# Seven-product FFN slabs with weight sums kept in device memory

## What is computed

```python
def swiglu_2(h, w_in, w_out):
    gate, up = jnp.split(h @ w_in, 2, axis=-1)
    return (jax.nn.silu(gate) * up) @ w_out

# block 1 of the first model (its FFN result is gated by the modulation, then the final norm follows)
x = x + mod_l[5] * swiglu(modulate(rmsnorm(x, ffn_norm_g[i]), mod_l[3], mod_l[4]), ffn_w1[i], ffn_w3[i], ffn_w2[i])
# a layer of the second model
x = x + 0.5 * swiglu_2(rms_norm(x, ffn1_norm[l]), ffn1_w_in[l], ffn1_w_out[l])
```

## Time and profile before

| | |
|---|---|
| Runs of before | 1642.88 us (1642.75 to 1643.07) |
| Profiled execution | 1642.93 us, span 1641.6 us |
| TensorE busy in the span | 1619.2 us (99%) |
| VectorE, ScalarE, GpSimd busy | 75%, 52%, 18% |
| DMA | 346 MB, 211 GB/s in the mean |
| TensorE clock granted | full |

### The profile page before, as it was taken

One profiled execution on the slowest core, in us unless ns is written; L12 is line 12 of the kernel. 1 busy time (PEld: TensorE's weight loads), 2 busy tenths in 40 slices (PEclk: granted clock), 3 DMA queues, 4 the chain that ended last, 5 costly groups with the idle time before them and its releaser, 6 DMA issues.

```text
span 1641.6 us, 21147 instructions
## 1 busy us (share of the span) xinstructions
PE 1619.2 (99%) x7872; PEld 1309.4 (80%) x7872; DVE 1226.6 (75%) x1476; ACT 850.7 (52%) x1062; POOL 292.8 (18%) x429
## 2 busy tenths in 40 slices
PE   6999999999999999999999999999999999999999
PEld 3776788888778888788888878888888888888887
DVE  3898778897787674766978776688667978866686
ACT  3436654435475443645656554454545647564453
POOL 0001000000002240134403002450044204003350
PEclk9999999999999999999999999999999999999999
DMA  9784398898638876577665428766676664347661
GB/s 350 242 289 169 106 318 278 309 353 264 205 123 268 272 251 196 175 232 225 200 189 180 129 80 248 224 198 220 200 215 211 216 199 158 103 129 233 215 212 52
DMA packets 250295, 346.22 MB, mean 211 GB/s; under 512 B 16160, under 2 KB 197124, under 8 KB 250192
## 3 DMA queue, kind: packets, MB, share of 16 engines
q1 hardware_dynamic: 236288, 323.00, 59.8%
q0 software_dynamic: 11472, 17.34, 4.5%
q10 hardware_dynamic: 2432, 4.51, 0.8%
HBM read 329.32 MB, written 1.05 MB: 201 GB/s over the span
## 4 chain that ended last, share of the span: by engine, by line
PE 89%; DVE 5%; ACT 3%; issue 1%; DMA 1%; SPq 0%; DVEq 0%; ACTq 0%
PE bank L491 21%; PE bank L493 21%; PE bank L492 21%; PE bank L898 5%; PE bank L903 5%; PE bank L899 5%; DMA raw<-in_ada_w 1%; DVE lo L2059 1%; PE bank L1411 1%; PE bank L1412 1%; PE bank L1414 1%; PE bank L846 1%; PE bank L1219 1%; ACT hi L1467 1%; DVE XN L2545 1%
## 5 line engine op out<-in xcount | busy, mean ns | idle before, releaser
L2059 DVE TENSOR_TENSOR lo<-raw,hi 128x2048 fp32r<-128x2048 f32 x230 | 528.2, 2300 | 194.2 <-ACT hi L1467 193.9
L1467 ACT ACTIVATE hi<-raw 128x2048 fp32r<-128x2048 f32 x242 | 462.0, 1914 | 248.0 <-PE bank L493 173.0
L491 PE MATMUL bank<-hi,XTh 128*128 128x512 f32 (+1 forms) x1424 | 558.8, 392 | 1.7 <-DVE XTl L2216 1.3
L493 PE MATMUL bank<-hi,XTl 128*128 128x512 f32 (+1 forms) x1424 | 551.4, 387 | 0.0
L492 PE MATMUL bank<-lo,XTh 128*128 128x512 f32 (+1 forms) x1424 | 550.9, 387 | 0.0
L491 PEld LDWEIGHTS bank<-hi,XTh 128*128 128x128 f32 x1424 | 267.4, 188 | 65.9 <-issue 12.5
L493 PEld LDWEIGHTS bank<-hi,XTl 128*128 128x128 f32 x1424 | 267.4, 188 | 55.2
L492 PEld LDWEIGHTS bank<-lo,XTh 128*128 128x128 f32 x1424 | 267.6, 188 | 53.8 <-issue 1.0
L3153 POOL DMA_DIRECT2D HTR<-BLK x320 | 192.4, 609 | 624.7 <-DVE BLK L2647 585.2
L898 PE MATMUL bank<-hi,HTh 128*128 128x512 f32 x400 | 156.6, 391 | 0.0
L899 PE MATMUL bank<-lo,HTh 128*128 128x512 f32 x400 | 155.7, 389 | 0.0
(11 more groups left out here) (420 smaller groups left out, 1862.8 us busy)
## 6 DMA issues: line engine op xcount, KB each, us to landing
raw<-in_ffn_w_in SPq DMA_DIRECT2D x176, 512.0 KB, 4.9
raw<-in_ffn_w SPq DMA_DIRECT2D x132, 512.0 KB, 5.0
raw<-in_ada_w SPq DMA_DIRECT2D x96, 512.0 KB, 5.5
raw<-in_ffn_w_out SPq DMA_DIRECT2D x88, 512.0 KB, 4.1
raw<-in_w_mix_in SPq DMA_DIRECT2D x52, 512.0 KB, 4.7
raw<-in_od_pw_w SPq DMA_DIRECT2D x24, 512.0 KB, 6.2
HTR<-BLK POOLq DMA_DIRECT2D x240, 48.0 KB, 3.9
raw<-in_ev_w_in SPq DMA_DIRECT2D x20, 512.0 KB, 9.8
```

The costliest lines, as they stand in the source:

```text
L491: pe.matmul(dst, xh, wh, start=start, stop=False)
L493: return pe.matmul(dst, xl, wh, start=False, stop=stop)
L1467: act.activation(hi[r][:, :], raw[g % RAW][:, :], ACT.Copy).then_inc(*up("hi", d))
L2059: dve.tensor_tensor(lo[r][:, :], raw[g % RAW][:, :], hi[r][:, :].bitcast(F32), ALU.subtract).then_inc(*up("lo", d))
```

## The change

- `FAST` takes in p = 2, the gated FFN ahead of the final norm, and `FASTS` becomes (0, 1, 3, 4, 6, 7): six of eleven down slabs in five FFNs, 30 slabs in place of 16.
- The weight sums no longer come from VectorE. GpSimd's queue makes them in a new buffer in device memory, `A["sums"][p]`, for each slab by six DMAs: two copies of 512 KB from the weight, then two accumulating DMAs of 256 KB from the weight, then one of 256 KB from the buffer to itself, then another one. Two slabs form a batch, and GpSimd waits for each of the four steps of each batch. The new function `weights_sums(p)` on GpSimd is called for p = 2 after the Fourier weights' DMAs, for p = 3 and 5 after the convolution's constants and ahead of `move_blocks(2)`, and for p = 6 and 8 after GpSimd's part of the mixers, ahead of `move_blocks(3l+5)`.
- The sums become slabs of their own in the weight stream (`sums_slab`), split like others, each behind its weight slab, which now leaves one quarter out (`fast_slab`). A down stage has 17 slabs in the stream in place of 11. SyncE waits for `sums_made` ahead of such a slab.
- `seven` uses two ring slots, with `used` raised after 9 and after 12 matmuls. The signs of the scheme change. `shared_sums` moves behind the splits of the last fast slab, and for p = 2 multiplies by the gate (`shared_added`).
- The places of the splits of `HTR` change (`FAST_SPLIT_UP`, `FAST_SPLIT_DOWN`); `SR`, `SL`, `SH` get new places in SBUF.

The diff, cut to its core:

```diff
     "hg_logs": "hg_e hg_ln hg_sig hg_z",
     "hg_squares": "hg_rows hg_sq hg_std hg_silu",
...
@@ -154,10 +155,27 @@
             return [(d[:, k, :], w[(2 * s + k) * P:(2 * s + k + 1) * P, :]) for k in range(2)]
         add(parts)
 
-    def down(name, w):
+    def fast_slab(w, s):
+        def parts(slot):
+            d = slot[:, :].rearrange("p (k n) -> p k n", k=2)
+            return [(d[:, 0, 0:512], w[2 * s * P:(2 * s + 1) * P, 0:512]), (d[:, 1, :], w[(2 * s + 1) * P:(2 * s + 2) * P, :])]
+        add(parts)
+
+    def sums_slab(p, i):
+        def parts(slot):
+            return [(slot[:, n * D:(n + 1) * D], A["sums"][p][i, :, n * D:(n + 1) * D]) for n in range(2)]
+        add(parts)
+
+    def down(name, w, p=None):
         first[name] = len(dense)
         for s in range(w.shape[0] // (2 * P)):
-            down_slab(w, s)
+            if p in FAST and s in FASTS:
+                fast_at[len(dense)] = FFNS[p], FASTS.index(s)
+                fast_slab(w, s)
+                sums_at[len(dense)] = p
+                sums_slab(p, FASTS.index(s))
+            else:
+                down_slab(w, s)
 
     def wide_slab(w, c0):
         v = row_tiles(w)
...
@@ -281,10 +299,11 @@
 SPLIT_UP = {5: (0, 1), 6: (2,), 8: (3, 4), 9: (5,), 10: (6,)}
 SPLIT_DOWN = {0: (7,), 1: (8,), 4: (9, 10)}
 
-FAST = (3, 5, 6, 8)
-FASTS = (1, 3, 5, 7)
-FAST_SPLIT_UP = {5: (0,), 6: (1, 2), 8: (4,), 9: (3, 5), 10: (6,)}
-FAST_BATCH = {n: [i for i, s in enumerate(FASTS) if s in batch] for n, batch in enumerate(BATCHES)}
+FAST = (2, 3, 5, 6, 8)
+FASTS = (0, 1, 3, 4, 6, 7)
+FAST_SPLIT_UP = {5: (2,), 6: (0, 1), 8: (5,), 9: (3, 4)}
+FAST_SPLIT_DOWN = {1: (8,), 2: (6, 7), 4: (9, 10)}
+FAST_BATCH = {n: [i for i, s in enumerate(FASTS) if s in batch] for n, batch in enumerate(BATCHES[:3])}
 FAST_COLUMNS = {6: 0, 9: 1}
 GAINS = {3: "ffn1_0", 4: "mix2_0", 5: "ffn2_0", 6: "ffn1_1", 7: "mix2_1", 8: "ffn2_1"}
 
...
@@ -440,11 +459,10 @@
         CAUSAL = tile_at("CAUSAL", [P, P + FOX_H], tmp_at + 4096)
 
         TR = tile_at("TR", [P, SLAB], tmp_at)
-        SR = tile_at("SR", [P, len(FASTS), 4, P], tmp_at + 8192)
-        SL = tile_at("SL", [P, len(FASTS), 4, P], tmp_at + 8192, F32R)
-        SH = tile_at("SH", [P, len(FASTS), 4, P], gate_at, F32R)
-        TH = XTh[:, :, :].rearrange("p k s -> p (k s)")
-        TL = XTl[:, :, :].rearrange("p k s -> p (k s)")
+        SR = tile_at("SR", [P, 8, 4, P], tmp_at)
+        SL = tile_at("SL", [P, 8, 4, P], tmp_at, F32R)
+        SH = [tile_at(f"SH{n}", [P, 2, 4, P], (gate_at, gate_at + 4096, scr_at)[n], F32R) for n in range(3)]
+        SHG = [tile_at(f"SHG{n}", [P, 2, 4, P], (tmp_at + 4096, cst_at, scr_at)[n], F32R) for n in range(3)]
         SUMS2 = SG[:, :, :].rearrange("p t n -> p (t n)")
 
         vec = A["vec"]
...
@@ -860,31 +904,32 @@
-                    return SH[:, i, n, :], SL[:, i, n, :]
+                    return sums_high_at(f, batch)[:, i - FAST_BATCH[batch][0], n, :], SL[:, sums_slot(i), n, :]
...
+                    pe.wait_ge(*at("hidden", (f, NC - 2, 1)))
+                three(bank[2][:, :], *x(0, 0), *w(0, 0), begin, end)
+                pe.wait_ge(*at("s_hi", (f, batch)))
+                pe.wait_ge(*at("s_lo", (f, batch)))
+                three(acc[0][1][:, :], *x_sum(3), *w(1, 1), begin, False).then_inc(*up("used", d))
+                ready(d + 1)
+                three(bank[3][:, :], *x_sum(0), *w_sum(0), begin, end)
+                three(acc[1][0][:, :], *x(1, 1), *w_sum(2), begin, False)
                 if begin:
                     pe.wait_ge(*at("hidden", (f, NC - 1, 1)))
-                three(bank[2][:, :], *x(0, 0), *w(0, 0), begin, end)
-                pe.wait_ge(*at("s_hi", (f, next(n for n in FAST_BATCH if i in FAST_BATCH[n]))))
-                pe.wait_ge(*at("s_lo", (f, next(n for n in FAST_BATCH if i in FAST_BATCH[n]))))
-                three(acc[0][1][:, :], *x_sum(3), *w(1, 1), False, False)
-                pe.wait_ge(*at("t_hi", (f, i)))
-                pe.wait_ge(*at("t_lo", (f, i)))
-                three(bank[3][:, :], *x_sum(0), *w_sum(0), begin, end)
                 three(bank[1][:, :], *x_sum(2), *w_sum(1), begin, end)
-                three(bank[0][:, :], *x_sum(1), *w_sum(2), begin, end)
-                return three(acc[1][0][:, :], *x(1, 1), *w_sum(3), False, False)
+                three(bank[0][:, :], *x_sum(1), *w_sum(3), begin, end).then_inc(*up("used", d + 1))
 
             def down(p, xh, xl, late, order=None, before=None, after=None, head=None):
                 nslab, d = DOWNS[p][0], first[f"down{p}"]
                 order = order or range(nslab)
 
                 def products(s, t, parts=(0, 1)):
-                    r = (d + s) % RING
+                    r = down_at(p, s) % RING
                     for n in range(2):
                         kk = 2 * order[s] + n
...
                 def moved_in_down(s):
-                    if p in FAST and s == 0:
+                    if p in FAST and s == 2:
                         sums_high(f, 2)
-                    for n in SPLIT_DOWN.get(s, ()):
+                    for n in (FAST_SPLIT_DOWN if p in FAST else SPLIT_DOWN).get(s, ()):
                         moved_high(n)
...
@@ -2058,51 +2091,39 @@
                     return
                 dve.tensor_tensor(lo[r][:, :], raw[g % RAW][:, :], hi[r][:, :].bitcast(F32), ALU.subtract).then_inc(*up("lo", d))
 
-            def weights_sums(f, d, i):
-
-                g = dense[d + FASTS[i]]
-                w = raw[g % RAW]
-                dve.wait_ge(*at(f"landed{g % RAW}", (g, 1)))
-                if i:
-                    dve.wait_ge(*at("t_lo", (f, i - 1)))
-                dve.tensor_tensor(TR[:, 0:D].rearrange("p (k n) -> p k n", k=2),
-                                  w[:, :].rearrange("p (k n) -> p k n", k=2)[:, :, 512:D],
-                                  w[:, 0:D].rearrange("p (k n) -> p k n", k=2), ALU.subtract).then_inc(*up("t_part", (f, i, 0)))
-                dve.wait_ge(*at("t_part", (f, i, 0)))
-                dve.tensor_tensor(TR[:, D:D + 512], w[:, D + 512:SLAB], TR[:, 0:512], ALU.subtract).then_inc(
-                    *up("t_part", (f, i, 1)))
-                dve.wait_ge(*at("t_part", (f, i, 1)))
-                dve.tensor_tensor(TR[:, D + 512:SLAB], w[:, D:D + 512], TR[:, D:D + 512], ALU.subtract).then_inc(
-                    *up("t_sum", (f, i)))
-
-            def weights_low(f, i):
-
-                dve.wait_ge(*at("t_hi", (f, i)))
-                dve.tensor_tensor(TL, TR[:, :], TH.bitcast(F32), ALU.subtract).then_inc(*up("t_lo", (f, i)))
-
             def sums_low(f, n):
 
-                own = slice(FAST_BATCH[n][0], FAST_BATCH[n][-1] + 1)
...
+
+            def shared_added(f, t):
+
+                sums = TR[:, t * D:(t + 1) * D]
+                if f == FFNS[2]:
+                    dve.wait_ge(*at("gate_full", (*FFN_GATE[2], 1)))
+                    dve.tensor_tensor(sums, sums, GATE[:, 1, :], ALU.mult).then_inc(*up("e_gated", (f, t)))
+                    dve.wait_ge(*at("e_gated", (f, t)))
+                    dve.tensor_tensor(X[:, t, :], X[:, t, :], sums, ALU.add).then_inc(*up("e_added", (f, t)))
+                else:
+                    dve.scalar_tensor_tensor(out=X[:, t, :], in0=sums, scalar=0.5, in1=X[:, t, :], op0=ALU.mult,
+                                             op1=ALU.add).then_inc(*up("e_added", (f, t)))
 
...
-                    if late is not None and s == 0:
+                for j, s, n in down_order(p)[:-3]:
+                    if late is not None and j == d:
                         late()
-                    if f is not None and s in FASTS[:-1]:
-                        weights_low(f, FASTS.index(s) + 1)
-                    if f is not None and s == FASTS[-1]:
-                        shared_sums(f)
-                    split(d + s + RING)
-                    if f is not None and s + RING in FASTS[2:]:
-                        weights_sums(f, d, FASTS.index(s + RING))
-                    if after:
+                    split(j + RING)
+                    if after and n == 0:
                         after(s)
+                if p - 1 in FAST:
+                    shared_sums(FFNS[p - 1])
...
@@ -3106,6 +3117,35 @@
                 ffn(3 * l + 5)
 
         def gpsimd_engine(pool):
+            def weights_sums(p):
+
+                l, kind = (p - 3) // 3, "ffn1" if p in (3, 6) else "ffn2"
+                w = A["ffn_w2"][1, :, :] if p == 2 else A[f"{kind}_w_out_2"][l, :, :]
+                w = w.rearrange("(s k p) n -> s k p n", k=2, p=P)
+                for n, own in FAST_BATCH.items():
+                    for i in own:
+                        v = A["sums"][p][i, :, :]
+                        pool.dma_start(v[:, 0:D], w[FASTS[i], 0, :, :]).then_inc(*up("sums_part", (p, i, 0), 16))
+                        pool.dma_start(v[:, D:SLAB], w[FASTS[i], 1, :, :]).then_inc(*up("sums_part", (p, i, 1), 16))
```

(52 more changed lines are left out.)

133 lines of the change are left out of this document (59 added, 74 removed).

## The result

The changed kernel takes 1764.41 us in median (1763.54 to 1774.48, 4 runs) against 1642.97 us (1642.75 to 1643.08) of the kernel before on the same chip: ratio 1.0753, 95% interval 1.0715 to 1.0792. The forecast was 1670 us, the range ended at 1707. The profiled execution is the 1774.48 us one, the longest of the four; what follows on it therefore adds up to 10 us more than the median shows, and no run shows why it was the longer one.

The account below looks back on a forecast made before the run. The prediction took TensorE, busy for 99% of the span, as the bound; -9.5 + 0 + 0.6 + 4.0 + 1 + 0 + 31 = +27.1 on 1642.93 us gave 1670 us, range 1637.5 to 1707.

Parts of the forecast that it names:

- Products: Down stages: three matmuls less in each of 14 slabs, 42 x 0.2267 us less on TensorE, -9.5 us.
- ends of the stages: Ends of down stages: later residual, 0.2 us in each of three, +0.6; p = 2's new gated shared sums, +4.0.
- stream: Down stages' doubled slab stream: keeps up thanks to nine slabs in store, 0, bounds 0 and +3 us.
- The threshold: Sums ahead of `move_blocks(2)`: ending by 543 us costs nothing, each us later costs one; room 147 us.
- The size of the sums of p = 3 and 5: GpSimd's sums from 396.5 us: 185 us long, bounds 117 and 253, ending at 574, a stall of 31 us.
- The price with the engines free: Sums of p = 3 and 5 as if alone: bytes at 370 GB/s, 68 + 49 = 117 us.
- The load: Weight stream beside the sums of p = 3 and 5: leaves them half the DMA engines, 136 + 49 = 185 us.
- Rival (d): Sums of p = 3 and 5: accumulations at double cost, stall 50 to 90 us, 1689 to 1729 us; chance 17%.
- The sums of p = 2: GpSimd's sums from about 136 us: 76 us, to 212 us, costing +1, lower bound 0, upper +6 us.
- The sums of p = 6 and 8: GpSimd's sums from 906.2 us, repeated in the second layer: 88 us, 119 at double cost; both fit, 0.
- Rival (e): Down stages: doubled slab stream starves TensorE, so the change brings nothing there, 1642 to 1649 us; chance 3%.

Follow-up runs that it names:

- e1: Changed kernel without the sums' DMAs and the waits for them, sums slabs loaded from the weight itself (results not the reference's): 1638.51 us, ratio 0.9972.
- e7: e1 with p = 2 left out of `FAST`, so four FFNs and no sums made: 1637.68 us, ratio 0.9967.
- e2: Changed kernel with the accumulating DMAs of the sums made plain copies of the same bytes, same waits: 1702.05 us, one run.
- e3: Changed kernel with all six slabs of an FFN in one batch, 4 waits for an FFN in place of 12: 1701.49 us, ratio 1.0362.
- e4: Changed kernel without weights_sums(5), p = 5 reading the sums of p = 3 (result not the reference's): 1660.68 us, ratio 1.0107.
- e6: Changed kernel with only weights_sums(3) moved, from 396 us to behind the convolution's constants at 276 us: 1698.51 us, ratio 1.0334.
- e8: Changed kernel with the edits of e6 and e3 together, five FFNs: 1683.78 us, ratio 1.0249.
- e9: e5 with each set of sums in the original three batches instead of one: 1659.57 us, ratio 1.0101.
- e11: Changed kernel, five FFNs, one batch each, sums of p = 3 behind the moves of p = 2, tile 1's shared addition deferred: 1655.42 us, ratio 1.0077.
- e5: Changed kernel with p = 2 out of `FAST`, sums of p = 3 in its place at 137 us, one batch per FFN: 1638.21 us, ratio 0.9971.

## Why the prediction was wrong

**Products, ends of the stages, stream** (-9.5, +0.6, +4.0, 0): right. Together they were -4.9; e1, which is this part by itself, measured 1638.5 - 1643.0 = -4.5. The wait at the end of down3 was 3.8 us in e1, 4.0 foreseen. The +0.6 for the other ends was not seen: e7, with 24 matmuls less and no p = 2, is 5.4 us below the kernel before, which is 24 x 0.2267 alone. So a part of the agreement is luck, as the lower clock behind the 3.8 us wait (some 1.8 us) was in no term. No wait stood within a down stage.

**The threshold** (what ends by 543 us costs nothing, each us later costs one): right. With a start 6.3 us later by then, it gives 663.5 - 543 - 6.3 = 114 us; the wait was 111.8. In e2 it gives 60.5, and the wait was 58.8; in e3, with TensorE 10.6 us behind, 50.3 against 47.7. In e4 the moves at 544.96 cost 1.4 us.

**The size of the sums of p = 3 and 5: this step failed.** It took 185 us, bounds 117 and 253; it was 260.7, outside both. The step had two factors, and it was wrong in the one that I thought safe:

- *The price with the engines free.* The lower bound was 68 us of engine time and 49 us of waits between steps, 117. The undisturbed batch gives 6 x 23.0 = 138 and 6 x 13.8 = 83, 221 us. As plain copies it is 92 and 65, 157. So both terms were about half of what they are; for copies alone they would have been three quarters, and the accumulation adds 64.
- *The load.* I had let it add 185 / 117, 58%. It added 261 / 221, 18%, so this factor was too high and hid a part of the other's error: the three batches of p = 3, beside the stream of weights, took 147 us, 49 each (33% above the undisturbed 36.8), and the three of p = 5, during which TensorE soon stood, 114, 38 each.

With 221 in place of 117, and no load at all, the same working would have had the sums end at 617.5, a stall of 74 us and 1713 us, outside my range. I had put the rate of loads into the cores' memory, many at once (370 GB/s), on copies and additions within device memory, of which four are in flight before the next step waits.

By the Trainium skill's fit for a GpSimd DMA ("DMA: Bandwidth & Descriptors", "Anatomy of one DMA") the prediction estimated 106 us for this work; the trace says 261, and copies alone took 207, or 157 at the pace of the undisturbed batch. So here the measurement decides against its use for copies within device memory, and not only because of the stream beside them (the prediction kept the fit for transfers that are alone; the page sets no such condition, and the undisturbed batch does not follow it either).

**Rival (d)**, accumulations at double cost, named the right mechanism (1.9 times the engine time for the second step, as it assumed), but started from a copy and a wait that were priced too low, so its own 1689 to 1729 ended 35 us short.

**The sums of p = 2** (+1, bounds 0 and 6): 4.1 us of waits and a clock of 0.98, 6.3 us by the start of the convolution, just above the bound. They took 133 us, not 76, and reached to 269.83, deep into the stretch at 0.91.

**The sums of p = 6 and 8** (0): 128 and 125 us against 88 foreseen and 119 at most. They ended at 1156.54 and 1643.34 and cost 7.7 us of waits.

**The sum** for the profiled execution, from e1: 1638.5 + 6.3 + 111.8 + 7.7 = 1764.3; 10.2 us remain to 1774.5. The stretches at a lower clock behind the waits account for about that: 0.87 from 678 to 700 us (2.9 us), 0.83 from 780 to 800 (3.4, of which e1 has 1.8 at the same place of the work), 0.97 and 0.95 from 1160 to 1200 (1.6) and 0.83 from 1660 to 1680 (3.4), and 1.3 us more of wait at the end of down3. The other executions of the same kernel, 10 us shorter, have no trace, so this division holds for the profiled one alone.

**Rival (e)**, the starved stream, was given 3% for the down stages. There it did not occur, but e3, e6, e8, e9 and e11 show it elsewhere, and the changed kernel too, for the 4.1 us at L1075. What stays open is the point from which it decides: in e5 a share of 1.04 from 400 to 480 us cost nothing, in e11 1.07 from 640 to 680 us cost 10 us. What the stream itself needs there differs (in e1, without sums, the share is 0.52 in the first stretch and 0.79 from 620 to 720 us), and so does how long the sums last: where the stream needs 0.9, from 205 us on, the last 32 us of a set cost 0.4 us in e5, and a second whole set behind the first cost 34 us in e8. That fits a store of slabs that is used up, but no run varied it alone.

The Trainium skill ("DMA: Bandwidth & Descriptors", section "Queues, rings and completion order") has each DMA engine go round between the queues with work; by that the stream loses where it needs more than its turn, which e11 (9.7 us late at 1.07) bears out in direction; no run measured the two queues' parts.

## What to carry to other kernels

Price a chain of dependent DMAs by its steps, each from issue to landing, and don't take the rate of another kind of transfer for it; if no row shows the operation, let the upper bound reach several times the lower. Work put on an idle engine's queue costs by what stands behind it in that queue, so place it by the due time of the next entry, issue it in few steps with many transfers each (e3 shows that this also presses harder on the other queues), and give up the part (here the fifth FFN, worth nothing even for free) that does not fit. Moving it earlier helps only into a stretch where the DMA engines have room.
